# In-projection first, memory keys and values made between its pairs

## What is computed

```python
z = rmsnorm(x, norm1_g) @ w_in                        # x: 2048 x 1024, w_in: 1024 x 2816
y_rwkv = rwkv7_group(z[..., :1792], ...)              # starts with the shift h + (h of the row before - h) * mu
y_sgu  = sgu_group(z[..., 1792:], ...)                # starts with gelu
x = x + concat([y_rwkv, y_sgu]) @ w_out
m = rmsnorm(mem, mem_norm_g)                          # mem: 256 x 1024
k, v = m @ wk, m @ wv                                 # the memory's keys and values
x = x + softmax(q(x) k^T / 16) v @ wo
x = x + (silu(h @ w_gate) * (h @ w_up)) @ w_down
return rmsnorm(x, norm_f_g)
```

## Time and profile before

| | |
|---|---|
| median of three runs | 3337.18 us |
| the profiled execution | 3342.77 us, its span 3340.6 us |
| TensorE busy | 3164.9 us, 95% of the span |
| VectorE (DVE) busy | 1191.2 us, 36% |
| GpSimd (POOL) busy | 1083.0 us, 32% |
| ScalarE (ACT) busy | 807.0 us, 24% |
| mean granted TensorE clock | 0.967 |

### The profile page before, as it was taken

One profiled execution on the slowest core, in us unless ns is written; L12 is line 12 of the kernel. 1 busy time (PEld: TensorE's weight loads), 2 busy tenths in 40 slices (PEclk: granted clock), 3 DMA queues, 4 the chain that ended last, 5 costly groups with the idle time before them and its releaser, 6 DMA issues.

```text
span 3340.6 us, 61874 instructions
## 1 busy us (share of the span) xinstructions
PE 3164.9 (95%) x26586; PEld 2640.6 (79%) x26586; DVE 1191.2 (36%) x1364; ACT 807.0 (24%) x1129; POOL 1083.0 (32%) x567
## 2 busy tenths in 40 slices
PE   6989999689899899999999999999999999999997
PEld 6768788578788788778888888877868888888885
DVE  4532552466666533223221221244232321222223
ACT  4102212234444331322311111122141321111111
POOL 6233222233435345134222222265305322222225
PEclk9989999798988889999999999999999999999998
DMA  5252222221222221101111111134201111111112
GB/s 177 96 185 82 77 99 100 70 58 40 51 59 57 60 89 44 57 26 50 45 49 50 46 49 50 47 103 151 72 16 38 50 50 44 50 50 45 50 50 76
DMA packets 130759, 222.36 MB, mean 67 GB/s; under 512 B 43792, under 2 KB 84752, under 8 KB 129808
## 3 DMA queue, kind: packets, MB, share of 16 engines
q1 hardware_dynamic: 130576, 219.60, 20.9%
HBM read 181.81 MB, written 37.75 MB: 66 GB/s over the span
## 4 chain that ended last, share of the span: by engine, by line
PE 73%; DVE 4%; issue 2%; POOL 1%; ACT 0%; POOLq 0%; DVEq 0%; ACTq 0%
PE ps L1046 55%; PE ps L1113 2%; PE ps L1277 2%; PE ps L1275 2%; PE ps L1480 2%; PE ps L1501 2%; PE ps L1259 2%; PE ps L1229 1%; DVE tu L1639 1%; PE ps L1356 1%; DVE normed L1961 1%; PE ps L1185 1%; PE ps L1217 1%; POOL sq L496 1%; PE ps L1162 1%
## 5 line engine op out<-in xcount | busy, mean ns | idle before, releaser
L487 POOL TENSOR_TENSOR w_lo<-w_raw,w_hi 128x1024 fp32r<-128x1024 f32 x244 | 595.6, 2442 | 1816.7 <-ACT w_hi L686 1815.4
L1046 PE MATMUL ps<-a_hi,w_hi 128*128 128x512 f32 x2368 | 929.1, 392 | 23.8 <-POOL w_lo L487 13.7
L1046 PE MATMUL ps<-a_lo,w_hi 128*128 128x512 f32 x2368 | 925.6, 391 | 0.0
L1046 PE MATMUL ps<-a_hi,w_lo 128*128 128x512 f32 x2368 | 732.4, 391 | 0.0
L686 ACT ACTIVATE w_hi<-w_raw 128x1024 fp32r<-128x1024 f32 x244 | 258.4, 1060 | 1761.4 <-PE ps L1046 1590.9
L1046 PEld LDWEIGHTS ps<-a_hi,w_hi 128*128 128x128 f32 x2368 | 447.3, 189 | 120.2 <-issue 24.5
L1046 PEld LDWEIGHTS ps<-a_lo,w_hi 128*128 128x128 f32 x2368 | 447.2, 189 | 93.9 <-issue 1.2
L1046 PEld LDWEIGHTS ps<-a_hi,w_lo 128*128 128x128 f32 x2368 | 447.0, 189 | 93.5
L1046 PE MATMUL ps<-b_hi,w_hi 128*128 128x512 f32 x1216 | 475.0, 391 | 3.0 <-POOL w_lo L487 2.1
L1046 PE MATMUL ps<-b_lo,w_hi 128*128 128x512 f32 x1216 | 473.1, 389 | 0.0
L1046 PE MATMUL ps<-b_hi,w_lo 128*128 128x512 f32 x1216 | 374.3, 389 | 0.0
(11 more groups left out here) (210 smaller groups left out, 3395.6 us busy)
## 6 DMA issues: line engine op xcount, KB each, us to landing
w_raw<-in_weights SPq DMA_DIRECT2D x244, 512.0 KB, 3.6
zT<-z_out SPq DMA_DIRECT2D x44, 512.0 KB, 2.8
in_raw<-in_xT SPq DMA_DIRECT2D x8, 1024.0 KB, 8.6
suv<-zT SPq DMA_DIRECT2D x16, 512.0 KB, 4.7
x<-in_xT SPq DMA_DIRECT2D x16, 512.0 KB, 5.7
outT<-normed SPq DMA_DIRECT2D x16, 512.0 KB, 3.5
zin<-zT SPq DMA_DIRECT2D x48, 128.0 KB, 2.4
zin<-zT SPq DMA_DIRECT2D x96, 64.0 KB, 2.3
```

The source lines that it names most:

```text
L487: pool.tensor_tensor(w_lo[:, u, :, :], w_raw[:, u, :, :], w_hi[:, u, :, :].bitcast(F32), ALU.subtract).then_inc(S["w_lo_done"], 1)
L1046: mm = pe.matmul(slot(u)[:, nb, 0:w], wt[:, u, k, :], r[:, k, nb * w:(nb + 1) * w], start=(k == 0 and r is hi_in and wt is w_hi), stop=(k ...
```

## The change

The in-projection's pairs of the first half come first. Memory pairs 0 to 5 stand one behind each of in-projection pairs 0 to 5, memory pairs 6 and 7 behind in-projection pair 10, at the change of halves. SP loads x before the memory, x of the second half already behind pair 3, and the constants in the second half. The memory norm has its own buffers (`sumsq_m`, `sq_m`, `rstd_m`), squares and factor, and mem_raw another place. POOL's squares for the second half come one tile behind each of pairs 7 to 14. The a_hi and a_lo tiles of the second half are made beside memory pairs 6 and 7. The transposes of v are put around the second job of the second half, and DVE's masks behind its eighth pair.

The diff, cut to its core:

```diff
-Q_IN = PAIRS_MEM
-Q_TAIL = Q_IN + HALVES * PAIRS_IN
+MEM_WITH = 6
+FIRST_HALF = [p for i in range(MEM_WITH) for p in (("in", i), ("mem", i))]
+FIRST_HALF += [("in", i) for i in range(MEM_WITH, PAIRS_IN)] + [("mem", i) for i in range(MEM_WITH, PAIRS_MEM)]
+Q_IN1 = len(FIRST_HALF)
+Q_TAIL = Q_IN1 + PAIRS_IN
...
-        mem_raw = place("mem_raw", [P, KT, MEM], F32, OS + 12 * KB)
+        mem_raw = place("mem_raw", [P, KT, MEM], F32, OX + 8 * KB)
+        sumsq_m = place("sumsq_m", [P, MEM], F32, Z_END + 8 * KB)
+        sq_m = place("sq_m", [P, MEM], F32, Z_END + 9 * KB)
+        rstd_m = place("rstd_m", [P, MEM], F32, Z_END + 10 * KB)
...
+            load_x(0, 0)
+            load_job(0, 0, ROW_IN)
+            load_x(0, 1)
+            load_job(0, 1, ROW_IN)
+            load_x(0, 2)
+            load_x(0, 3)
             sp.dma_start(mem_raw[:], memT.rearrange("k p t -> p k t")).then_inc(S["act_in"], 16)
-            load_pair(0, 0, first=True)
...
-            load_x(0, 0)
-            for i in range(1, 4):
-                load_pair(i, 2 * i)
-                load_x(0, i)
-            with sp.Fori(4, PAIRS_MEM) as i:
-                load_pair(i, 2 * i)
-            load_pair(Q_IN, ROW_IN)
-
+            for pair in range(1, Q_IN1):
+                kind, i = FIRST_HALF[pair]
+                load_pair(pair, 2 * i if kind == "mem" else ROW_IN + 2 * i)
+                if pair == 3:
+                    sp.wait_ge(S["act_lo"], KT)
+                    sp.wait_ge(S["sumsq_done"], KT)
+                    for j in range(4):
+                        load_x(1, j)
+                kind, i = FIRST_HALF[pair - 1]
+                if kind == "in":
+                    store_z(0, i)
+            load_pair(Q_IN1, ROW_IN)
+            load_pair(Q_IN1 + 1, ROW_IN + 2)
             sp.wait_ge(S["kv_done"], 8)
             sp.wait_ge(S["v_trc"], 4)
             sp.dma_start(kT_d, kT0[:].rearrange("p k t -> p (k t)")).then_inc(S["kv_store"], 16)
             sp.dma_start(v_d, v0[:].rearrange("p k t -> p (k t)")).then_inc(S["kv_store"], 16)
...
-                load_and_store(1, 4)
-                if hf == 0:
-
-                    sp.wait_ge(S["act_lo"], 2 * KT)
-                    sp.wait_ge(S["sumsq_done"], 2 * KT)
-                    for j in range(4):
-                        load_x(1, j)
-                    load_and_store(4, 6)
...
+            store_z(1, 0)
+            load_pair(Q_IN1 + 2, ROW_IN + 4)
+            sp.wait_ge(S["kv_store"], 32)
...
+            store_z(1, 1)
+            with sp.Fori(3, PAIRS_IN) as i:
+                load_pair(Q_IN1 + i, ROW_IN + 2 * i)
+                store_z(1, i - 1)
+            store_z(1, PAIRS_IN - 1)
...
+            for pair in range(1, Q_IN1):
+                split_pair(pair)
+                k = pair - 7
+                if 0 <= k < KT:
+                    pool.wait_ge(S[f"in{k // 2}"], 32)
+                    if k == 0:
+                        pool.wait_ge(S["stat_ps"], 1)
+                    square_tile(in_raw[:, k, :], (k, KT + k), k == 0)
+            for i in range(3):
...
+            for k in range(2):
+                split_square(k)
+                hi(0, k, True)
+            for k in range(2, KT):
+                split_square(k)
+            act.wait_ge(S["act_in"], 16)
+            for k in range(KT):
+                act.activation(mem_hi[:, k, :], mem_raw[:, k, :], ACT.Copy, scale=gain[:, G_MEM, k:k + 1]).then_inc(S["m_hi"], 1)
+            hi(1, 0)
+            split_rms(0)
+            act.wait_ge(S["m_stat"], 1)
+            act.activation(rstd_m[:], ps[:, 6, 0:MEM], ACT.Sqrt, bias=eps[:, 0:1], scale=1.0 / D).then_inc(S["m_root"], 1)
+            hi(1, 1)
+            for pair in range(2, Q_IN1 - 1):
+                kind, i = FIRST_HALF[pair - 1]
+                for u in range(2):
+                    hi(pair, u)
+                    if kind == "in" and i >= SHIFT_TILES // 2 and pair < Q_IN1 - 2:
+                        gelu(0, i, u)
+            gelu(0, PAIRS_IN - 1, 0)
+            act.wait_ge(S["job_done"], 2 * (Q_IN1 - 2))
+            for j in range(4):
+                act.wait_ge(S[f"in{j}"], 32)
+            next_hi(range(2))
+            gelu(0, PAIRS_IN - 1, 1)
+            hi(Q_IN1 - 1, 0)
+            next_hi(range(2, 4))
+            hi(Q_IN1 - 1, 1)
+            next_hi(range(4, 6))
+            hi(Q_IN1, 0)
+            next_hi(range(6, KT))
+            hi(Q_IN1, 1)
+            act.wait_ge(S["job_out"], 2 * Q_IN1)
+            split_rms(1)
...
+            for pair, (kind, i) in enumerate(FIRST_HALF):
+                for u in range(2):
+                    if kind == "mem":
+                        job(pair, u, mem_hi, mem_lo, KT, MEM, lo_wait=(lambda k: pe.wait_ge(S["m_lo"], k + 1)) if i == 0 and u == 0 else None)
+                        continue
+                    job(pair, u, a_hi, a_lo, KT, first=pair == 0, lo_wait=split(0) if pair == 0 and u == 0 else None)
+                    if pair == 0 and u == 0:
+                        stats(0)
+                        pe.wait_ge(S["m_sum"], KT)
+                        pe.matmul(ps[:, 6, 0:MEM], ones, sumsq_m[:], start=True, stop=True).then_inc(S["m_stat"], 1)
+            job(Q_IN1, 0, a_hi, a_lo, KT, lo_wait=split(KT))
+            stats(1)
+            pe.wait_ge(S["job_out"], 2 * Q_IN1)
+            turn_mem(0)
+            turn_mem(1)
+            job(Q_IN1, 1, a_hi, a_lo, KT)
+            turn_mem(2)
+            turn_mem(3)
...
+            for k in range(KT):
+                x_lo(0, k)
+                if k:
+                    dve.wait_ge(S["sqa_done"], k + 1)
+                if k == 1:
+                    dve.tensor_tensor(sumsq[:], z_out[:, 0, :], z_out[:, 1, :], ALU.add).then_inc(S["sumsq_done"], 2)
+                elif k:
+                    dve.wait_ge(S["sumsq_done"], k)
+                    dve.tensor_tensor(sumsq[:], sumsq[:], z_out[:, k % 2, :], ALU.add).then_inc(S["sumsq_done"], 1)
+            for k in range(KT):
+                dve.wait_ge(S["m_hi"], k + 1)
+                dve.scalar_tensor_tensor(mem_lo[:, k, :], mem_raw[:, k, :], gain[:, G_MEM, k:k + 1],
+                                         mem_hi[:, k, :].bitcast(F32), ALU.mult, ALU.subtract).then_inc(S["m_lo"], 1)
+            root_to_rstd(0)
+            dve.wait_ge(S["m_root"], 1)
+            dve.reciprocal(rstd_m[:], rstd_m[:]).then_inc(S["m_rstd"], 1)
+            dve.wait_ge(S["m_rstd"], 1)
+            for pair, (kind, i) in enumerate(FIRST_HALF):
                 for u in range(2):
-                    dve.wait_ge(S["job_done"], 2 * i + u + 1)
-                    dve.tensor_tensor(dst[:, k + u, :], slot(u)[:, 0, 0:MEM], rstd[:, 0:MEM], ALU.mult).then_inc(S["job_out"], 1)
-
-                x_lo(0, i)
-                if i:
-                    dve.wait_ge(S["sqa_done"], i + 1)
-                if i == 1:
-                    dve.tensor_tensor(sumsq[:], z_out[:, 0, :], z_out[:, 1, :], ALU.add).then_inc(S["sumsq_done"], 2)
-                elif i:
-                    dve.wait_ge(S["sumsq_done"], KT + i)
-                    dve.tensor_tensor(sumsq[:], sumsq[:], z_out[:, i % 2, :], ALU.add).then_inc(S["sumsq_done"], 1)
-            dve.wait_ge(S["job_out"], 2 * PAIRS_MEM)
+                    if kind == "mem":
+                        memory(pair, i, u)
+                        if i >= MEM_WITH:
+                            for k in range(4 * (i - MEM_WITH) + 2 * u, 4 * (i - MEM_WITH) + 2 * u + 2):
+                                x_lo(1, k)
+                    elif i < SHIFT_TILES // 2:
+                        z_tile(0, pair, i, u, True)
+                    else:
+                        plain_tile(0, pair, i, u)
...
+            root_to_rstd(1)
+            for g in range(2):
                 dve.wait_ge(S["v_tr"], g + 1)
+                dve.tensor_copy(v0[:, 0, g * BANK:(g + 1) * BANK], ps[:, 6 + g, :]).then_inc(S["v_trc"], 1)
+            z_tile(1, Q_IN1, 0, 0, True)
+            for g in range(2):
+                dve.wait_ge(S["v_tr"], g + 3)
+                dve.tensor_copy(v0[:, 1, g * BANK:(g + 1) * BANK], ps[:, 6 + g, :]).then_inc(S["v_trc"], 1)
             dve.wait_ge(S["v_trc"], 4)
+            z_tile(1, Q_IN1, 0, 1, True)
...
+            for i in range(SHIFT_TILES // 2, PAIRS_IN):
+                for u in range(2):
+                    plain_tile(1, Q_IN1 + i, i, u)
+                    if u and i == PAIRS_IN - 4:
+                        masks()
+                    if u and i == PAIRS_IN - 3:
+                        spatial()
```

More of the change, by code:

```diff
@@ new lines, in gelu, with next_hi @@
+            def gelu(hf, i, u):
+                m = 2 * i + u
+                act.wait_ge(S["z_ext_done"], hf * IN_TILES + m + 1)
+                act.wait_ge(S[f"z_st{u}"], 16 * (1 + hf * PAIRS_IN + i))
+                act.activation(z_out[:, u, :], z_ext[:, u, 1:TB + 1], ACT.Gelu_apprx_tanh).then_inc(S["z_out_done"], 1)
+            def next_hi(tiles):
+                for k in tiles:
```

(44 more changed lines are left out.)

254 lines of the change are left out of this document (78 added, 176 removed).

## The result

On the same chip the changed kernel took 3369.27 us (median of four, 3364.62 to 3376.45) and the kernel before 3334.66 (3324.86 to 3339.1): a ratio of 1.011, interval 1.008 to 1.0139, so 34.6 us slower, 27 to 46. The profiled execution has a span of 3367.8 us.

What follows compares the result with a forecast made beforehand. TensorE was taken as the bound, so order matters only where it waits or runs at half clock. The second half's end moves from 605.9 to 656.4, +50.5 us, put on median 3337.18: 3388 us (3376 to 3400; range 3363 to 3404).

Steps and rivals of the forecast that it cites:

- Sign and place: Slower (0.91); TensorE waits for w_lo six times behind memory pairs, 8 to 11 us each, a seventh ahead of mem7.
- rival A: Same mechanism with shorter latency, weight tile ready at T + 12.5 in each turn: 3364 to 3376 us; chance 0.17.
- The turns: in1 to in5, each with a memory pair: 39.8 us a turn, five 199 us, plus 4.2 for POOL's squares.
- The latency: From T, the in pair's end, to the next split weight tile: T + 15.3, its load behind the z store.
- S: Start of in1, after in0 and mem0: 73.4 us, bounds 65 and 79.
- B: Rival with long latency or clock: 17.3 in each turn and S = 79, 3400 to 3408 us; chance 0.12.
- in6 to in10 and the second half: 2.7 us of half clock plus 108.8, then 243.5 at full clock; no stall from x or the constants.
- The change of halves: mem6 and mem7 after in10's end T: mem7's weights ready at T + 16.2, second half starts at T + 24.8.
- the carry: Code after the in-projection is unchanged, so the +50.5 us at its end is carried to the kernel's end.
- The cause of the 5.99 us stall: First half, kernel before: x's four megabytes stood ahead of weights needed next; with the 7.71 us stall, 19 us go.
- the constants' stall: First half, kernel before: 7.71 us from the constants' loads ahead of a weight load; said to go.
- Rival C: Next in pair's load in place when the memory pair ends: turns 28.5 us, in1 at 62, 3305 us; chance 0.06.

Runs made afterwards that it cites:

- E2: Changed kernel with the next pair's weight loads issued ahead of the z stores on SP at three of seven places, behind in0, in2 and in4; 3348.27 us, ratio 1.0062.
- B1: Kernel before, with the next pair's weight load issued on SP ahead of x of the second half and ahead of the constants; 3320.63 us, ratio 0.9976.
- E1: Changed kernel with weight loads of the pair after the memory pair issued ahead of the z stores on SP, at all seven places; 3327.82 us, ratio 0.9998.
- E7: E1 with memory squares later, second-half squares only behind in pairs, and DVE reading mem1 to mem5's first tile before z_out; 3291.00 us, ratio 0.9907.

## Why the prediction was right, and where it was not

- **Sign and place: right.** Six waits of 7.9 to 9.7 us behind memory pairs and a seventh ahead of mem7, ended by w_lo, ACT waiting for w_raw ahead of them, the load right behind the store of the second z tile. E2 shows the cause. 3369.27 lies in the range (3363 to 3404) but not in the forecast's own (3376 to 3400); the time is rival A's (3364 to 3376), though A's cause, a short latency, is not what made it.
- **The turns: right to 3 us.** 38.9, 38.2, 41.3, 41.0 and 40.8 are 200.1 us in all, for 199 + 4.2. The latency was T + 14.7 and 14.6, not 15.3: z_out ended at T + 5.9, and the load went out 0.4 us behind the store, not 0.9. The three larger turns are those with squares, where z_out ended at T + 7.4, as foreseen. S was 73.08 for 73.4, though the memory's squares on POOL, which were to end before 40, ended at 42.4 and TensorE waited 1.83 us for them; DVE's chain ended later still. A's T + 12.5 and B's 17.3 did not occur.
- **in6 to in10 and the second half: right.** 111.7 us for 111.5 and 243.6 for 243.5, no stall from x or the constants.
- **The change of halves: mis-sized.** From in10's end at 384.9 to 407.06 are 22.2 us, for 24.8. Mem7's first job starts at T + 13.8, not 16.2. Most of that is z_out: ACT's list took 5.1 us and not 7, so the last one ended at 390.00. The rest is the way from there to a ready tile, 8.6 us where I had taken 9.25 out of a row with a shift tile: SP issues the load at 390.43, ACT rounds at 395.15 and POOL subtracts at 396.28.
- **The sum and the carry.** 0.3 less at the start, 3.1 in the turns and 2.6 at the change of halves, 0.3 more in the two stretches at full clock: the in-projection's end moved by 44.7 where 50.5 was forecast. "I carry the difference at that point to the end" gave +34.6 in the first comparison, +46.3 and +42.2 in the two others. Over these three the step is about right; the first profile of before was long in the mixers, and the sum stood on that one execution. So of the 18.7 us between 3388 and 3369.27, 5.8 are the terms above; 2.5 are the kernel before, 3334.66 now for 3337.18; and 10.1 are the difference between 44.7 and the 34.6 of this comparison, which the two others don't repeat.
- **The cause of the 5.99 us stall: half of it.** "The 5.99 us stall was x's four megabytes ahead of weights that were needed next" names what came last in the kernel before, but by 0.4 us only. B1 took it away, and the stall stayed, at 7.95: POOL's square waited for x, with the weight's subtraction behind it. The step was drawn from SP's issue order alone and didn't ask what else waited for the same megabytes. Its result held, since in the changed order no such stall appeared, and the constants' stall was as told.
- **Rival C was sound, and its price nearly so.** With the load in place E1 still met two waits that were not in the sum. Only E7 reaches turns of 29.1; its in1 starts at 61.90 (C said 62) and its last z_ext starts at 577.26 (C: 574).

## To carry to other kernels

When short work is put between long work on the engine that bounds, ask of each queue which loads stand behind stores or waits of the long part; the cover that hid them is the time until next use, and it shrinks from two long jobs to one short pair. And list what is late second and third ahead of a repair, since it gets only the difference to the next: the row names the one that came last, and the one behind it can be 0.4 us away, in the releaser's own list. A change that brings work earlier may also put it beside other work that it stretches, as POOL's split did to z_out in E1.
